# The ups of a second FFN as 512-wide products, with a sum of two half banks on VectorE

## What is computed

```python
def swiglu(h, w13, w2):
    a, b = jnp.split(h @ w13, 2, axis=-1)
    return (jax.nn.silu(a) * b) @ w2

x = x + 0.5 * g3x * swiglu(modulate(rmsnorm_2(x, norm_ffn2[l]), sh3x, sc3x), w13_ffn2[l], w2_ffn2[l])
```

## Time and profile before

| | |
|---|---|
| runs (3), median | 2193.01 us (2190.12 to 2193.04) |
| the profiled execution | 2190.08 us, span 2188.3 us |
| mean granted TensorE clock | 0.988 |
| TensorE matmul busy | 2124.7 us, 97% |
| TensorE weight load busy | 1840.0 us, 84% |
| VectorE busy | 1219.0 us, 56% |
| ScalarE busy | 977.2 us, 45% |
| GpSimd busy | 125.4 us, 6% |

### The profile page before, as it was taken

How to read it: one execution, slowest core, us unless ns; L and a number is a source line. 1 busy time by engine, 2 the same in 40 slices (tenths; PEclk the granted TensorE clock), 3 DMA queues, 4 the chain that set the end, 5 groups by cost and what they waited for, 6 DMA issues and landing times.

```text
span 2188.3 us, 35852 instructions
## 1 busy us (share of the span) xinstructions
PE 2124.7 (97%) x12658; PEld 1840.0 (84%) x12658; DVE 1219.0 (56%) x2086; ACT 977.2 (45%) x1406; POOL 125.4 (6%) x65
## 2 busy tenths in 40 slices
PE   8999999999999999999999999999999999999998
PEld 6898999557888888888888888787888888998997
DVE  4457796886666666666665333224544533455553
ACT  4644554224555555555554222213333444346653
POOL 0000687000000000000000000000000000000000
PEclk9999999999999999999999999999999999999999
DMA  6344344886555555555543232222323335354552
GB/s 222 127 135 164 127 162 157 308 306 220 192 191 185 189 191 184 189 204 191 185 163 114 97 96 96 96 96 72 108 94 106 111 130 162 116 183 141 176 191 96
DMA packets 95559, 343.25 MB, mean 157 GB/s; under 512 B 10914, under 2 KB 12450, under 8 KB 95108
## 3 DMA queue, kind: packets, MB, share of 16 engines
q1 hardware_dynamic: 94388, 337.28, 46.4%
q0 software_dynamic: 1104, 5.05, 0.7%
HBM read 341.24 MB, written 1.05 MB: 156 GB/s over the span
## 4 chain that ended last, share of the span: by engine, by line
PE 91%; DVE 4%; ACT 2%; POOL 1%; DMA 1%; issue 1%; ACTq 0%; DVEq 0%; SPq 0%
PE ps L1399 16%; PE ps L1401 15%; PE ps L1400 15%; PE ps L1628 8%; PE ps L1642 5%; PE ps L1644 5%; PE ps L1643 5%; PE ps L1630 4%; PE ps L1430 2%; PE ps L1431 2%; PE ps L1432 2%; PE ps L1603 2%; PE ps L1579 2%; PE ps L1782 1%; POOL WL L390 1%; DMA RAW<-in_wstream 1%
## 5 line engine op out<-in xcount | busy, mean ns | idle before, releaser
L831 DVE TENSOR_TENSOR WL<-RAW,WH 128x1024 fp32r<-128x1024 f32 x519 | 627.2, 1224 | 506.9 <-ACT WH L419 503.6
L419 ACT ACTIVATE WH<-RAW 128x1024 fp32r<-128x1024 f32 x565 | 585.0, 1052 | 288.4 <-PE ps L1401 159.8
L1399 PE MATMUL ps<-XH,WH 128*128 128x256 f32 (+1 forms) x1200 | 384.6, 321 | 7.3 <-DVE XL L848 5.4
L1400 PE MATMUL ps<-XL,WH 128*128 128x256 f32 (+1 forms) x1200 | 379.1, 316 | 0.0
L1401 PE MATMUL ps<-XH,WL 128*128 128x256 f32 (+1 forms) x1200 | 379.0, 316 | 0.0
L1628 PE MATMUL ps<-XHL,WH 128*128 128x512 f32 x752 | 268.5, 397 | 0.0
L1399 PEld LDWEIGHTS ps<-XH,WH 128*128 128x128 f32 x1200 | 229.1, 191 | 26.6 <-issue 5.4
L1400 PEld LDWEIGHTS ps<-XL,WH 128*128 128x128 f32 x1200 | 229.3, 191 | 15.3 <-issue 1.0
L1401 PEld LDWEIGHTS ps<-XH,WL 128*128 128x128 f32 x1200 | 229.2, 191 | 14.5
L1399 PE MATMUL ps<-XHL,WH 128*128 128x256 f32 x696 | 205.1, 295 | 17.6 <-DVE XHL L846 7.8
L1630 PE MATMUL ps<-XHL,WL 128*128 128x256 f32 x752 | 210.9, 280 | 0.0
(11 more groups left out here) (276 smaller groups left out, 3126.2 us busy)
## 6 DMA issues: line engine op xcount, KB each, us to landing
RAW<-in_wstream SPq DMA_DIRECT2D x637, 512.0 KB, 3.3
H<-in_xT SPq DMA_DIRECT2D x1, 1024.0 KB, 4.9
CTX<-in_ctxT POOLq DMA_DIRECT2D x1, 1024.0 KB, 5.5
HX<-in_ctxT POOLq DMA_DIRECT2D x1, 1024.0 KB, 6.1
DIST<-in_dist POOLq DMA_DIRECT2D x1, 1024.0 KB, 5.2
out<-HX SPq DMA_DIRECT2D x2, 512.0 KB, 3.1
MASK<-in_mask POOLq DMA_DIRECT2D x1, 512.0 KB, 4.0
DFTL<-in_dftl POOLq DMA_DIRECT2D x1, 512.0 KB, 4.0
```

What stands on the lines that cost most here:

```text
L419: act.activation(WH[:, slot, :], RAW[:, slot, :], ACT.Copy).then_inc(hi_ready, 1)
L831: dve.tensor_tensor(WL[:, slot, :], RAW[:, slot, :], WH[:, slot, :].bitcast(F32), ALU.subtract).then_inc(lo_ready, 1)
L1399: pe.matmul(dst, wh, xh, start=start, stop=False, skip_group_check=not check)
L1400: pe.matmul(dst, wh, xl, start=False, stop=False, skip_group_check=not check)
```

## The change

XH2 and XL2, neighbours already, become the two halves of one tile XHL2. The ups of the second FFN use `wide_chunk` in place of `feature_chunk`: for each of 8 groups one 512-wide product of WH with both halves, and one 256-wide product of WL with XH2 onto the first half of the bank. A bank then holds wh xh + wl xh in its first 256 columns and wh xl in the other 256. VectorE adds them with a `tensor_reduce` per bank: bank a into TA, bank b into HT. ScalarE takes the silu in place in TA, after the sum of a (`a_sum`), and VectorE multiplies TA and HT, both now in SBUF. The first FFN (n == 0) is left as it is.

```diff
-        XH2 = sb("XH2", [P, KB * 2 * T], REG, dt=F32R)
-        XL2 = sb("XL2", [P, KB * 2 * T], dt=F32R)
+        XHL2 = sb("XHL2", [P, 2, KB * 2 * T], REG, dt=F32R)
+        XH2, XL2 = XHL2[:, 0, :], XHL2[:, 1, :]
...
 # ScalarE, up_block
-                    act.wait_ge(chunk_done, at(c + 1, 4, it))
-                    act.activation(TA[:, f, 0:width], ps[:, 2 * f, 0:width],
-                                   ACT.Silu).then_inc(s["ffn_silu"], 1)
+                    if n == 0:
...
+                    else:
+                        act.wait_ge(s["a_sum"], at(f + 1, 2, it))
+                        act.activation(TA[:, f, 0:T], TA[:, f, 0:T], ACT.Silu).then_inc(s["ffn_silu"], 1)
...
 # VectorE, up_block
-                    dve.wait_ge(chunk_done, at(c + 2, 4, it))
-                    dve.wait_ge(s["ffn_silu"], at(n * FF + i0 + f + 1, 2, it))
-                    dve.tensor_tensor(HT[:, f, 0:width], TA[:, f, 0:width], ps[:, 2 * f + 1, 0:width],
-                                      ALU.mult).then_inc(s["ffn_prod"], 1)
+                    if n == 0:
...
+                    else:
+                        for b, (dst, summed) in enumerate(((TA, s["a_sum"]), (HT, s["b_sum"]))):
+                            dve.wait_ge(chunk_done, at(c + b + 1, 4, it))
+                            dve.tensor_reduce(dst[:, f, 0:T], ps[:, 2 * f + b, :].rearrange("p (a t) -> p t a", a=2),
+                                              AXX, ALU.add).then_inc(summed, 1)
+                        dve.wait_ge(s["b_sum"], at(f + 1, 2, it))
+                        dve.wait_ge(s["ffn_silu"], at(FF + f + 1, 2, it))
+                        dve.tensor_tensor(HT[:, f, 0:T], TA[:, f, 0:T], HT[:, f, 0:T],
+                                          ALU.mult).then_inc(s["ffn_prod"], 1)
...
 # TensorE
+            def wide_chunk(c, bank, it, norm):
+
+                split_ready(c, it, 4)
+                both = ps[:, bank, :].rearrange("p (a t) -> p a t", a=2)
+                for k in range(KB):
+                    if norm is not None:
+                        pe.wait_ge(s["norm_lo"], SPLIT_NORM[norm] * KB + k + 1)
+                    w = slice(k * P, k * P + P)
+                    pe.matmul(both, WH[:, c % 4, w], XHL2[:, :, k * T:k * T + T], start=(k == 0), stop=(k == KB - 1),
+                              skip_group_check=True)
+                    ins = pe.matmul(ps[:, bank, 0:T], WL[:, c % 4, w], XH2_8[:, k, :], start=False, stop=(k == KB - 1),
+                                    skip_group_check=True)
+                ins.then_inc(chunk_done, 1)
...
-                        feature_chunk(upc + 2 * i0 + j, ps[:, j, 0:width], xh, xl, it, 4,
-                                      norm=N_FFN2 if n and not j else None)
+                        if n == 0:
+                            feature_chunk(upc + 2 * i0 + j, ps[:, j, :], xh, xl, it, 4)
+                        else:
+                            wide_chunk(upc + j, j, it, None if j else N_FFN2)
```

More of the change, by code:

```diff
@@ L702, in up_block @@
                         split_hi(c + 3, it, 4)
-                    act.wait_ge(chunk_done, at(c + 1, 4, it))
-                    act.activation(TA[:, f, 0:width], ps[:, 2 * f, 0:width],
-                                   ACT.Silu).then_inc(s["ffn_silu"], 1)
+                    if n == 0:
+                        act.wait_ge(chunk_done, at(c + 1, 4, it))
+                        act.activation(TA[:, f, :], ps[:, 2 * f, :], ACT.Silu).then_inc(s["ffn_silu"], 1)
+                    else:
+                        act.wait_ge(s["a_sum"], at(f + 1, 2, it))
+                        act.activation(TA[:, f, 0:T], TA[:, f, 0:T], ACT.Silu).then_inc(s["ffn_silu"], 1)
                     act.wait_ge(s["ffn_prod"], at(n * FF + i0 + f + 3, 2, it))
@@ L1234, in up_block @@
                         split_lo(c + 3, it, 4)
-                    dve.wait_ge(chunk_done, at(c + 2, 4, it))
-                    dve.wait_ge(s["ffn_silu"], at(n * FF + i0 + f + 1, 2, it))
-                    dve.tensor_tensor(HT[:, f, 0:width], TA[:, f, 0:width], ps[:, 2 * f + 1, 0:width],
-                                      ALU.mult).then_inc(s["ffn_prod"], 1)
+                    if n == 0:
+                        dve.wait_ge(chunk_done, at(c + 2, 4, it))
+                        dve.wait_ge(s["ffn_silu"], at(i0 + f + 1, 2, it))
+                        dve.tensor_tensor(HT[:, f, :], TA[:, f, :], ps[:, 2 * f + 1, :],
+                                          ALU.mult).then_inc(s["ffn_prod"], 1)
[7 more added lines that the diff above has]
+                        dve.tensor_tensor(HT[:, f, 0:T], TA[:, f, 0:T], HT[:, f, 0:T],
+                                          ALU.mult).then_inc(s["ffn_prod"], 1)
                     dve.wait_ge(s["ffn_hi"], at(n * FF + i0 + f + 1, 2, it))
```

## The result

| | before | after |
|---|---|---|
| median of the runs (6 each) | 2193.03 us | 2205.23 us |
| the profiled execution | 2190.08 us | 2205.24 us |
| ratio of the times | | 1.0068, 95% interval 1.0058 to 1.0079 |

The change makes the kernel 0.7% slower. The forecast was 2207 for the median, and 2205.0 for an execution like the profiled one of before. One of the six executions of before took 3495.21 us; it is a slow one that the ratio leaves out, and nothing on record explains it. The two medians alone would give 1.0056.

A forecast was written before the change was run, and what follows sets the result against it. TensorE was taken to bound the second FFN's ups, with the VectorE-ScalarE chain taking over after the change. The profiled 2190.08 plus 14.9 us gave 2205.0, and 2207 was predicted for the median, range 2200 to 2222.

The forecast's parts named there:

- The stage and its bound: Second FFN's ups: TensorE bounds at 11.52 us per iteration; the VectorE-ScalarE chain needs 10.48, leaving 1.04 of room.
- the rival that TensorE stays the bound: Ups: the reductions fit the chain's room, so not slower, 2187 to 2194 us; chance 0.08.
- TensorE's gain: Ups: a wide chunk takes 2.81 us against 2.88, 3.1 us less TensorE work, lost whole in the stall.
- The stall: Ups: TensorE waits 1.6 us per iteration, at the chunk whose weight remainder is late.
- The reduction's price: VectorE in the ups: each added reduction takes 0.69 us, the next one starting 0.61 later.
- The rival of strided pairs at half rate: VectorE's reductions: 2.1 us more per iteration, 23 in all, so about 2230 us; chance 0.03.
- The chain after: Ups, HIDH to HIDH: period 12.83 us, the chain growing by 2.35, of which 1.04 was covered by the old wait.
- The table load: ScalarE before TA: the load runs ahead of the wait; rival, it comes behind, 13 us more, 2220; chance 0.03.
- The clock: TensorE in the ups: the new 1.6 us gaps may bring some clock drops, costing 0 to 0.2 us each.
- the rival of two drops an iteration: TensorE's clock in the ups: 2.4 us lost against 1.6 of room, 9 more, 2216 us; chance 0.05.
- The end: End of the ups: last HIDH at 2122.75 against 2107.89, 14.9 us later, and nothing changes after the downs begin.
- the median: Whole kernel: 2207 us, between 2205.0 and 2207.9, as the earlier median lay 2.9 above the profiled execution.

The follow-up runs named there:

- wide kernel without sums: Changed kernel without both reductions, silu and product reading the first half of each bank (timing only); ratio to the kernel before 0.9999, ups 2.30 us shorter.
- narrow one with sums: Changed kernel with the three 256-wide products of before, both reductions kept (timing only); ratio to the kernel before 1.0076, ups 14.88 us longer.
- sum of a early: Changed kernel with bank a's reduction moved ahead of the block's two weight remainders on VectorE; ratio to the kernel before 1.0007, ups 2.92 us longer.
- version a block ahead: Changed kernel with each block preparing weights of the block after the next, behind silu and product; ratio to the kernel before 0.9986, ups 1.40 us shorter.

## Why the prediction was right, step by step

- **The stage and its bound.** Busy times alone (VectorE 58%, ScalarE 69%) would have hidden the reductions. The chain read in order of time gave 1.04 us of room. The wide kernel without sums shows that room directly (period 11.31 with 0.82 of waiting), and the narrow one with sums shows the chain's 12.83 without the wide form. So the rival that TensorE stays the bound is out.
- **TensorE's gain** was put at 3.1 us and measured at 2.3 (11.31 against 11.52, 11 times). The term was oversized: the mean chunk in the wide kernel is 2.83. The expert stage's 2.81 was no stray, its neighbours have it too (798.75 to 801.56, 809.94 to 812.75); inside such a chunk most pairs are 0.353 apart, as in the ups, and only the first, behind a product of another kind, takes 0.34. As forecast the gain was lost whole in the stall, so this error left no mark on the total; that is luck of the case, not accuracy.
- **The stall** was forecast at 1.6 us per iteration (12.83 less 11.24). By the periods it is 1.52 (12.83 less 11.31). In the trace the first product behind it starts 1.54 after the last one instead of 0.12 (2023.08 to 2024.62), and its pair then takes 0.46 instead of 0.35 (2024.62 to 2025.08).
- **The reduction's price**, 0.69 with the next 0.61 later, was 0.68 and 0.60. The rival of strided pairs at half rate is out.
- **The chain after**: forecast 12.83, measured 12.84. Product at 6.64 forecast and 6.65 measured, odd product 12.27 and 12.28. Two errors hide in it: TA came at 5.96, not 6.08, and the product stands 0.13, not 0.08, behind reduction b. The first has no effect while b is the longer. The second is made up by reduction a, which starts 0.02 earlier than forecast (5.24), and by the 0.01 each that the reductions and the step between them are shorter.
- **The table load** ran from 2011.43 to 2012.71 while its silu waited until 2013.50 for the sum. A load runs ahead of the wait, as the earlier trace rows had it, and that rival is out too.
- **The clock.** Over ten stretches of 12.8 us from 1993.8 on, the granted clock was 1.00 in each, with one gap in each, 1.24 to 1.38 us long before the product and up to 1.7 before its weight load. I had allowed for some drops, without cost. None came, and the rival of two drops an iteration is out. The gap of 3.7 us ahead of the downs was followed by one, as the 1.75 us were before. But the gap's length alone doesn't decide it: the 2.7 us of the sum of a early and the 2.15 of the version a block ahead were followed by 1.00. The changed kernel over 2124 to 2128 and the 4 us after:

```profile
2124.00:2128.00 4.00, 3.91 (x20) 3.91 (x21) 2.40 (x3) 1.45 (x2) 0.00 (x0) 0.58 0.44 139
2128.00:2132.00 4.00, 4.00 (x35) 4.00 (x34) 1.23 (x1) 1.42 (x2) 0.00 (x0) 0.99 0.53 200
```

- **The end.** The last HIDH was forecast for 2122.75 and came at 2123.05 in an execution whose ups began 0.21 later. The total of 2205.0 against 2205.24 is then 14.9 against 14.93 in the ups.
- **What was off** is the median: I added up to 2.9 us for the difference between the profiled execution and the median of three. The later executions of before spread over 2186 to 2196 with medians of 2190.1 and 2190.9, so I take the offset for chance of that small sample; that isn't shown. The 2207 missed by 1.8 us for this reason, not by the mechanism.

## What to carry to other kernels

Where two engines hand work to each other in each round, add up the chain of one round in order of time and compare it with the round of the engine that bounds; the difference is the room, and busy shares say nothing of it. Work added to the half-idle engine costs next to nothing ahead of a step that waits anyway, and its time, less what another engine's step hides, behind it: the same two reductions cost 14.9 us behind the weight remainders, 2.9 with one moved ahead, and nothing of TensorE's pace when the weights are prepared a block earlier. And a small gain on the bounding engine is kept only as far as the chain's room reaches.

## What the runs showed of the hardware

- A reduction of pairs that lie 1 KB apart in PSUM takes 681 to 685 ns for 512 inputs in the changed kernel (692 at most as a mean in any version), as much as the contiguous product on 512 of the earlier trace rows, 692.
- After a gap of TensorE ahead of the downs of 1.75 to 3.7 us the granted clock fell in seven of nine profiled executions; after gaps of 2.15 and 2.7 us in the other two it stayed 1.00, and the rest of the kernel took 1.5 us less.
- The step from reduction b to the product took 0.12 us in the loops and 0.03 in the written-out last blocks of the version a block ahead (2098.05 + 0.69 to 2098.77; its lines stand at the end). Both wait for the same semaphores, in the loop against values held in registers; that this is the cause I infer and haven't tested.
- A 512-wide and a 256-wide product together take 0.353 us (11.31 / 32), three 256-wide ones 0.360 (11.52 / 32, so 0.120 each). With a weight load for each, the 512-wide one thus costs 0.233, nearly two 256-wide ones.

```profile
2098.05 0.69 DVE L1257 TENSOR_REDUCE HT<-ps 128x256 f32<-128x512 f32 x1 [1.20 <-PE ps L1757]
2098.77 0.42 DVE L1261 TENSOR_TENSOR HT<-TA,HT 128x256 f32<-128x256 f32 x1
```
